# Loops written out and norm sums taken to GpSimd in a two-block transformer kernel

## The reference

```python
def rms_norm(x, g):
    x32 = x.astype(jnp.float32)
    y = x32 * lax.rsqrt(jnp.mean(x32 * x32, axis=-1, keepdims=True) + EPS)
    return (y * g.astype(jnp.float32)).astype(x.dtype)
...
for l in range(DEPTH):
    h = rms_norm(x, norm_g[l])
    ...
    x = x + merged @ w_out[l]
return rms_norm(x, final_g)
```

## Time and profile before

| | |
|---|---|
| median of 3 runs | 1506.96 us (1505.96 to 1507.57) |
| the profiled execution's own time | 1507.09 us |
| its span | 1505.3 us |
| granted TensorE clock, mean | 0.944 |
| busy: TensorE matmul, VectorE, ScalarE, GpSimd | 89%, 57%, 44%, 18% |

### The profile page before, as it was taken

One profiled execution on the slowest core, in us unless ns is written; L12 is line 12 of the kernel. 1 busy time (PEld: TensorE's weight loads), 2 busy tenths in 40 slices (PEclk: granted clock), 3 DMA queues, 4 the chain that ended last, 5 costly groups with the idle time before them and its releaser, 6 DMA issues.

```text
span 1505.3 us, 32278 instructions
## 1 busy us (share of the span) xinstructions
PE 1343.5 (89%) x12138; PEld 1277.6 (85%) x12138; DVE 859.4 (57%) x1352; ACT 669.0 (44%) x1067; POOL 263.7 (18%) x259
## 2 busy tenths in 40 slices
PE   4889989979899989889668889999999899799997
PEld 4879988979799978889557789989989799799997
DVE  4334745646445645655488967657656565555544
ACT  5324544443444435343434663333333353566633
POOL 0000040006000130134042226335334100000000
PEclk9979999999999989999889999999999899899999
DMA  5525452335434533344323332222222255355553
GB/s 187 190 74 169 153 181 100 111 112 163 140 126 135 187 121 117 98 139 142 123 73 109 115 124 75 95 80 69 87 76 77 88 184 162 115 182 181 191 182 130
DMA packets 59065, 194.32 MB, mean 129 GB/s; under 512 B 6248, under 2 KB 13928, under 8 KB 58736
## 3 DMA queue, kind: packets, MB, share of 16 engines
q1 hardware_dynamic: 49248, 179.33, 36.3%
q10 hardware_dynamic: 9440, 12.90, 2.5%
q0 software_dynamic: 304, 1.07, 0.2%
HBM read 189.06 MB, written 4.21 MB: 128 GB/s over the span
## 4 chain that ended last, share of the span: by engine, by line
PE 60%; issue 22%; DVE 8%; ACT 3%; DVEq 2%; POOL 1%; POOLq 1%; DMA 1%; ACTq 1%
PE stream_ps L278 16%; PE stream_ps L279 14%; PE stream_ps L280 14%; DVE w_lo L270 2%; DVE qkvT L1100 2%; PE free_ps L1640 2%; PE free_ps L1657 1%; ACT w_hi L264 1%; PE free_ps L1658 1%; DVEq L1106 1%; PE free_ps L356 1%; POOLq L408 1%; PE free_ps L1405 1%; DMA cst<-cst_dram 1%; DVE oT L363 1%
## 5 line engine op out<-in xcount | busy, mean ns | idle before, releaser
L278 PE MATMUL stream_ps<-h_hi,w_hi 128*128 128x256 f32 (+1 forms) x2016 | 600.2, 298 | 56.7 <-DVE w_lo L270 26.7
L270 DVE TENSOR_TENSOR w_lo<-raw,w_hi 128x1024 fp32r<-128x1024 f32 x342 | 432.9, 1272 | 347.3 <-ACT w_hi L264 342.1
L279 PE MATMUL stream_ps<-h_lo,w_hi 128*128 128x256 f32 (+1 forms) x2016 | 583.1, 289 | 0.0
L280 PE MATMUL stream_ps<-h_hi,w_lo 128*128 128x256 f32 (+1 forms) x2016 | 582.4, 289 | 0.0
L278 PEld LDWEIGHTS stream_ps<-h_hi,w_hi 128*128 128x128 f32 x2016 | 395.7, 196 | 68.8 <-issue 31.9
L280 PEld LDWEIGHTS stream_ps<-h_hi,w_lo 128*128 128x128 f32 x2016 | 395.9, 196 | 0.0
L279 PEld LDWEIGHTS stream_ps<-h_lo,w_hi 128*128 128x128 f32 x2016 | 395.0, 196 | 0.4 <-issue 0.2
L264 ACT ACTIVATE w_hi<-raw 128x1024 fp32r<-128x1024 f32 x342 | 358.0, 1054 | 62.1 <-PE stream_ps L280 55.6
L1224 DVE TENSOR_TENSOR xy<-xy,free_ps 64x128 f32<-64x128 f32 x180 | 44.7, 283 | 64.1 <-PE free_ps L1658 49.9
L795 ACT ACTIVATE n<-free_ps 64x128 f32<-64x128 f32 x80 | 22.0, 275 | 106.3 <-PE free_ps L1640 105.4
L1100 DVE SCALAR_TENSOR_TENSOR qkvT<-st_raw,gains,qkvT 128x272 f32<-128x272 f32 x96 | 65.7, 725 | 5.3 <-ACT qkvT L682 2.6
(11 more groups left out here) (327 smaller groups left out, 2142.4 us busy)
## 6 DMA issues: line engine op xcount, KB each, us to landing
raw<-stream_dram SPq DMA_DIRECT2D x342, 512.0 KB, 3.5
gate_spill<-gate_out ACTq DMA_DIRECT2D x16, 128.0 KB, 2.0
xT<-xT_dram ACTq DMA_DIRECT2D x1, 1088.0 KB, 8.6
stage<-wik_dram ACTq DMA_DIRECT2D x2, 544.0 KB, 4.2
mem_raw<-memT_dram ACTq DMA_DIRECT2D x1, 1024.0 KB, 5.0
hankel<-rel_scratch POOLq DMA_DIRECT2D x1, 1024.0 KB, 10.5
x_spill<-xT ACTq DMA_DIRECT2D x1, 1024.0 KB, 4.8
gb<-gate_spill ACTq DMA_DIRECT2D x1, 1024.0 KB, 5.8
```

What stands on the lines that cost most here:

```text
L270: nc.vector.tensor_tensor(w_lo[s][:, :, :], raw[:, s, :].rearrange("p (k n) -> p k n", k=KT), w_hi[s][:, :, :].bitcast(F32), ALU.subtract) ...
L278: nc.tensor.matmul(ps, l_hi, r_hi, start=first, stop=False)
L279: nc.tensor.matmul(ps, l_hi, r_lo, start=False, stop=False)
L280: return nc.tensor.matmul(ps, l_lo, r_hi, start=False, stop=last)
```

## The change

Every `Fori` loop becomes a Python loop, so that its body is written out once per pass and all addresses and semaphore values are constants. Nothing else in these bodies changes. Second, at five of the seven sums of squares GpSimd adds the squared tiles 1 to 7 into tile 0, each as soon as its square is there, and TensorE makes one product with the ones matrix in place of eight. These are the sums ahead of layer 0, between the layers, after layer 1, ahead of the gate and up matrices, and the last one. The sum over the memory and the 272-token sum ahead of the second block stay as they were.

```diff
+        sqsum_ready = sem("sqsum_ready")
...
+        def add_squares(pool, sq, sq_at):
+
+            for k in range(1, KT):
+                nc.gpsimd.drain()
+                pool.wait_ge(sq_ready, sq_at + k + 1)
+                op = nc.gpsimd.tensor_tensor(sq[:, 0, :], sq[:, 0, :], sq[:, k, :], ALU.add)
+            op.then_inc(sqsum_ready, 1)
+
+        def summed_squares(pe, sq, sums):
+
+            pe.wait_ge(sqsum_ready, sums)
+            nc.tensor.matmul(free_ps[0][:, 0:sq.shape[-1]], ones, sq[:, 0, :], start=True, stop=True).then_inc(ss_ready, 1)
+
...
         @block.sync
...
-            with sp.Fori(0, a["groups"]) as G:
+            for G in range(0, a["groups"]):
...
         @block.gpsimd
...
             pool.sem_inc(part_used, 2)
+            add_squares(pool, wideS, 8)
             pool.wait_ge(flip_done, HEADS)
...
-            with pool.Fori(0, LAYERS) as l:
+            for l in range(0, LAYERS):
...
-                with pool.Fori(0, 4) as hp:
+                for hp in range(0, 4):
...
                     nc.gpsimd.drain()
-
+                add_squares(pool, wideS, 16 + 8 * l)
...
-            with pool.Fori(0, STEPS) as t:
+            for t in range(0, STEPS):
...
                     op.then_inc(sdec_ready, 1)
+            add_squares(pool, wideS, 24 + 8 * LAYERS)
+            add_squares(pool, wideS, 32 + 8 * LAYERS)
...
         @block.tensor
...
-            with pe.Fori(0, LAYERS) as l:
+            for l in range(0, LAYERS):
...
-                sum_squares(pe, wideS, 1 + l, 8 + 8 * l)
+                summed_squares(pe, wideS, l + 1)
...
-            sum_squares(pe, wideS, 1 + LAYERS, 8 + 8 * LAYERS)
+            summed_squares(pe, wideS, LAYERS + 1)
             sum_squares(pe, wide, 2 + LAYERS, 16 + 8 * LAYERS)
...
-            with pe.Fori(0, GATE_STEPS) as t:
+            for t in range(0, GATE_STEPS):
...
-            sum_squares(pe, wideS, 3 + LAYERS, 24 + 8 * LAYERS)
+            summed_squares(pe, wideS, LAYERS + 2)
...
-            sum_squares(pe, wideS, 4 + LAYERS, 32 + 8 * LAYERS)
+            summed_squares(pe, wideS, LAYERS + 3)
```

More of the change, by code:

```diff
@@ L426, in _ @@
                     nc.gpsimd.tensor_copy(st_v, v[:, :, bass.ds(hp * P, P)]).then_inc(v_staged, 1)
-                with pool.Fori(0, 2) as mp:
+                for mp in range(0, 2):
                     pool.wait_ge(pv_done, 6 * l + 4 + mp + 1)
@@ L434, in _ @@
                 nc.gpsimd.drain()
-                with pool.Fori(0, 3) as br:
+                for br in range(0, 3):
                     for s in range(SLOTS):
@@ L595, in _ @@
                     evac(act, G + 8, s, mqT[:, s, :])
-                with act.Fori(0, 4) as hp:
+                for hp in range(0, 4):
                     for s in range(SLOTS):
@@ L613, in _ @@
                             op.then_inc(softT_ready, 1)
-                with act.Fori(0, 2) as mp:
+                for mp in range(0, 2):
                     for s in range(SLOTS):
@@ L631, in _ @@
                             op.then_inc(softT_ready, 1)
-                with act.Fori(0, 3) as br:
+                for br in range(0, 3):
                     for s in range(SLOTS):
@@ L640, in _ @@
                     nc.scalar.activation(hS_hi[:, ks, :], merged[:, ks, :], ACT.Copy, scale=0.5).then_inc(mhi_ready, 1)
-                with act.Fori(0, 2) as w:
+                for w in range(0, 2):
                     for s in range(SLOTS):
@@ L806, in step @@
                 fill(7)
-            with act.Fori(0, GATE_STEPS) as t:
+            for t in range(0, GATE_STEPS):
                 step(t, True)
@@ L840, in _ @@
             act.dma_start(xS, a["x_spill"][:, :, tok]).then_inc(x_back, 16)
-            with act.Fori(2, 4) as w:
+            for w in range(2, 4):
                 for s in range(SLOTS):
@@ L861, in _ @@
             split_norm_hi(2 * LAYERS + 4, hS_hi, oS)
-            with act.Fori(0, FT // 2) as w:
+            for w in range(0, FT // 2):
                 for s in range(SLOTS):
@@ L914, in _ @@
             dve.wait_ge(admit_in, 16)
-            with dve.Fori(0, LAYERS) as l:
+            for l in range(0, LAYERS):
                 G = G0 + LAYER_GROUPS * l
@@ L976, in split_y @@
                     return nc.vector.tensor_tensor(dst_lo, src, dst_hi.bitcast(F32), ALU.subtract)
-                with dve.Fori(0, 4) as hp:
+                for hp in range(0, 4):
                     for s in range(SLOTS):
@@ L1013, in _ @@
                 nc.vector.drain()
-                with dve.Fori(0, 2) as mp:
+                for mp in range(0, 2):
                     for s in range(SLOTS):
@@ L1032, in _ @@
                     nc.vector.drain()
-                with dve.Fori(0, 3) as br:
+                for br in range(0, 3):
                     for s in range(SLOTS):
@@ L1047, in _ @@
                                                    in1=hS_hi[:, ks, :].bitcast(F32), op0=ALU.mult, op1=ALU.subtract).then_inc(mlo_ready, 1)
-                with dve.Fori(0, 2) as w:
+                for w in range(0, 2):
                     for s in range(SLOTS):
@@ L1254, in step @@
                         op.then_inc(s_ready, 1)
-            with dve.Fori(0, GATE_STEPS) as t:
+            for t in range(0, GATE_STEPS):
                 step(t, True)
@@ L1305, in _ @@
             split_norm(3 + LAYERS, G_NORM2, 2 * LAYERS + 2, oS, xS, hS_hi, hS_lo)
-            with dve.Fori(0, FT // 2) as w:
+            for w in range(0, FT // 2):
                 for s in range(SLOTS):
@@ L1391, in _ @@
                     block_rows(pe, G + 3, s, act_evac, E + 12 + s + 1, hS_hi, hS_lo)
-                with pe.Fori(0, 5) as g:
+                for g in range(0, 5):
                     for s in range(SLOTS):
                         block_cols(pe, G + 4 + g, s, act_evac, E + 16 + 4 * g + s + 1, hS_hi, hS_lo)
-                with pe.Fori(0, 4) as hp:
+                for hp in range(0, 4):
                     pe.wait_ge(mask_ready, l + 1)
@@ L1430, in _ @@
                 mm.then_inc(mixed_done, 1)
-                with pe.Fori(0, 2) as mp:
+                for mp in range(0, 2):
                     pe.wait_ge(qk_staged, 6 * l + 4 + mp + 1)
@@ L1457, in _ @@
                     mm.then_inc(pv_done, 1)
-                with pe.Fori(0, 3) as br:
+                for br in range(0, 3):
                     pe.wait_ge(act_evac, SLOTS + E + ACT_EVACS)
@@ L1703, in _ @@
                     mm.then_inc(oss_done, 1)
-            with pe.Fori(0, 2) as w:
+            for w in range(0, 2):
                 for s in range(SLOTS):
@@ L1713, in _ @@
                 block_cols(pe, G_GU, s, dve_evac, D2 + 40 + s + 1, hS_hi, hS_lo)
-            with pe.Fori(1, FT // 2) as w:
+            for w in range(1, FT // 2):
                 for s in range(SLOTS):
```

1 line of the change is left out of this document (removed).

## The result

The changed kernel takes 1484.3 us (median of 4 runs, 1482.1 to 1486.6) against 1507.3 us: a ratio of 0.9845, 95% interval 0.9824 to 0.9866. The profiled pair shows 1486.55 against 1507.09 us. The forecast of 1499.4 us (1495.0 to 1505.0) had the sign, and a third of the size.

What follows compares the result with a forecast made beforehand. TensorE, busy for 89% of the span, was taken as the bound, so only its waits or half-clock stretches could shrink. Terms of 0.9 + 2.3 + 1.5 + 0 + 3.0 = 7.7 us gave 1499.4 us, range 1495.0 to 1505.0.

Steps and rivals of the forecast that it cites:

- Last norm: Norm at the kernel's end: shorter hops and one product of ones instead of eight gain 0.9 us.
- Norm between the layers: Norm between layers 0 and 1: earlier square and fewer products gain 2.3 us, with ScalarE's table load binding.
- First norm: Norm ahead of layer 0: adds hidden under the memory products, ScalarE's table load binding, gain 1.5 us.
- Norms after layer 1 and before gate and up: At these two norms the new add costs what the shorter cycle gives: zero each, between 0.3 gain and 0.8 loss.
- Hops elsewhere: Shorter hops at head pairs, memory attention and last merges gain 3.0 us together, bounds 0 and 5.
- The memory attention: Four waits behind register-addressed steps and a loop head on VectorE: up to 0.6 us each, 1.8 together.
- The second rival: New GpSimd adds collide with VectorE's subtractions in the output products: 15.1 us lost, 1514.5 us; chance 0.06.
- The merges and f_lo: Shorter hops at the last merges, f_lo and the like: 0.6 us gained.
- Costed at nothing: Step loop, table loads, SP's queue, GpSimd's 35 adds and TensorE's longer straight code: no gain or loss counted.
- The hops' rival: Shorter hops give nothing anywhere, so their 3.0 us term is 0: 1502.4 us; chance 0.21.
- The clock's rival: TensorE's idle time ahead of norms is paid in half clock behind four norms, 6.8 us: 1506.2 us; chance 0.13.
- The returns' rival: Loop returns cost everywhere, so the step loop's three returns save 2.58 us each more: 1491.7 us; chance 0.02.

Runs made afterwards that it cites:

- e3: Kernel before with GpSimd's layer loop written out and a wait added so it clears the merged tile later; memory-pair loops kept: 1503.7 us, ratio 0.9984.
- e6: Kernel before plus the GpSimd sums, all loops kept except that over the five recurrent steps, which is written out on all four engines: 1508.8 us, ratio 1.0023.
- e11: Changed kernel with VectorE held back about 0.7 us before its copy into y_hi, so it meets GpSimd's clearing again: 1482.4 us, ratio 0.9858.
- e10: Kernel before with only the loops behind the recurrent steps written out (last W_br and W_out products, gate/up, down): 1502.2 us, ratio 0.9965.
- e1: Kernel before with all loops written out as in the change, but the eight products of ones kept, no GpSimd sums: 1485.1 us, ratio 0.9854.
- e14: Changed kernel with idle TensorE products, ones by ones, around the sums' waits and ahead of the head pairs: 1475.7 us, ratio 0.9780.
- e2: Kernel before with the GpSimd sums as in the change but every loop kept: 1529.4 us, ratio 1.0149.

## Why the prediction was right, and where it failed

1. *Last norm, 0.9:* 1.0 us (3.49 to 2.50).
2. *Norm between the layers, 2.3:* 2.38 us, and the closeness is in part luck. The sum had ScalarE's table load bind, 0.3 us behind the product; it ended 0.4 us ahead of it (404.51 against 404.92), 1.7 us behind the square's end and not 2.4. The product, 2.1 us behind the square, was as forecast, and the square came 0.5 us sooner, not 0.6.
3. *First norm, 1.5:* 1.94 us, with the table load binding, as said. Single executions hide it: the stretch around it is no shorter in after.
4. *Norms after layer 1 and before gate and up, 0 each:* 0.3 and 0.2 us later, the add on the path against the shorter cycle, as argued.
5. *Hops elsewhere, 3.0:* here it failed. The head pairs (0.1 each) are right. The memory attention, 1.8 us, measured 0.8 us a layer at the first transposes and 6.5 us a layer behind them, 14.7 us in all. That is 12.9 us over the forecast; the profiled pair misses 12.8 us in all, the medians 15. The step took each wait as a chain of hops "up to 0.6 each", and never asked why VectorE's steps there took as long as they did. In its own terms it priced the waits at 1.8 us, and they gave 8.1: 4.7 us of shorter steps at all the waits of the memory attention and not only at the four ahead of transposes, and 3.4 us of the clash, as e3 shows. The other 6.6 us are clock, which the step put at nothing, and whose cause stays open (e6, e11). Two signs stood in the trace of before: a copy of 2.14 us whose like took 0.43 in the next pair, and a clock of 0.89. The second rival weighed the very sharing of VectorE and GpSimd on the earlier trace rows, but only for the new adds against a subtraction; it wasn't asked whether an old clash would go. The merges and f_lo, 0.6, were short too: F and G gave 4.0 us, 1.0 of it the last norm.
6. *Costed at nothing:* the step loop (period 58.6 us, as before), SP's queue, GpSimd's adds in the output products (w_lo's subtractions have a mean of 1.27 us in both kernels) and straight code (96 fetches, no stall in it) were right, and so were the table loads as far as the runs tell: e10 takes them out of gate and up, and F is shorter by no more than its last wait.

The rivals: the collision didn't come in the output products, where the rival priced it. It came ahead of layer 0, where the seven adds run beside VectorE's subtractions: two of these take 3.35 us there, 2.44 in e1, and TensorE waits 3.12 us for them, 2.68 in e1. The hops' rival (nothing) fell. The clock's rival may have a true mechanism in it, by what e14 gained; in the change itself the clock gave more in the attention than it took at the norms. The returns' rival was rightly small for this placement, and its mechanism is real: with 63 instructions fewer ahead of the loop e2 pays 3 us a return.

## What to carry to other kernels

Look for one instruction that takes far longer than its like a pass later, and for what the other engine of the VectorE and GpSimd pair does just then: a clash that hangs on hundredths of a microsecond was worth 1.7 us of waiting in each layer here, beside 2.4 us for all the shorter steps together. Count the shorter steps at every wait of the stretch. Where a loop's body on TensorE is large, look at its instruction packets pass by pass; a harmless edit ahead of it can make every return cost 3 us, and a written-out loop is safe from that. Price what a shorter wait gives in TensorE's clock beside the wait itself, and read it by stretches, since single executions move by several microseconds.

## What the runs showed that was not expected

- A copy of 0.43 us took 2.14 us behind a GpSimd clearing of 1.81 us, which reads nothing; a subtraction beside the same clearing took its usual 0.69 us. The copy ended 0.28 us behind the GpSimd operation that it met, whether that was the clearing or a copy.
- Of two copies that started 0.05 and 0.07 us ahead of the clearing one lost and one won.
- A step body of about 1770 TensorE instructions is kept over four passes at one place of the program and fetched in each of them, nine packets, at another 63 instructions earlier (and 39 earlier).
- Idle products in waits of 5 to 7 us made the changed kernel some 0.7% faster.
- The same code ran A's first part in 31.1 or 28.0 us, at clocks of 0.89 and 1.00, with the same waits.
